# Conditioning tiles multiplied two stages earlier, norm rows loaded earlier, the decay chain later

## What is computed

```python
mod_lat = silu(c) @ w_ada + b_ada            # 12 tiles of 512 columns
mod_ctx = silu(c_ctx) @ w_ada + b_ada
sh_m, sc_m, gt_m, sh_f, sc_f, gt_f = split(mod_lat, 6)
u_ctx = ctx * (1 + csc_m) + csh_m            # only k and v are made of it
u_lat = x * (1 + sc_m) + sh_m
q, k, v, g, glu, gates = u_lat @ w_in + b_in
q, k = rope(q), rope(k)
# retention with decays exp(log_sigmoid(ret_decay)), state from k_c, v_c
y_a = (silu(g) * head_norm(o)) @ w_ret_out
z = silu(LN(depthwise_conv31(za * sigmoid(zb))))
y_b = z @ w_conv_out + b_conv_out
mix = (sigmoid(ga) * y_a + sigmoid(gb) * y_b) @ w_mix_out + b_mix_out
h = LN(ALPHA * x + gt_m * mix; ln1_g, ln1_b)
moe = sum over top 2 of 32 experts of (h * (1 + sc_f) + sh_f)
h = LN(ALPHA * h + gt_f * moe; ln2_g, ln2_b)
a_in = h * norm_pre_2 * row_scale            # into the second block
```

## Time and profile before

| | |
|---|---|
| median of 3 runs | 1579.76 us (1579.15 to 1589.21) |
| profiled execution | 1580.53 us, span 1578.7 us, mean granted clock 0.987 |
| PE busy | 1489.3 us (94%); weight loads 1030.8 |
| DVE, ACT, POOL busy | 715.5 (45%), 577.4 (37%), 415.5 (26%) |
| DMA | 381.18 MB, mean 241 GB/s |
| chain that ended last | PE 70%, DMA 12%, DVE 5%, POOL 4%, ACT 3% |

### The profile page before, as it was taken

The page is one execution under the profiler, slowest core; times in us unless marked ns, Lnnn a source line. Parts: engine busy times, 40 slices in busy tenths (PEclk is TensorE's granted clock), DMA queues, the critical chain, the costliest instruction groups (busy, mean ns, idle before and its releaser), DMA issues.

```text
span 1578.7 us, 22936 instructions
## 1 busy us (share of the span) xinstructions
PE 1489.3 (94%) x9454; PEld 1030.8 (65%) x9454; DVE 715.5 (45%) x1294; ACT 577.4 (37%) x781; POOL 415.5 (26%) x316
## 2 busy tenths in 40 slices
PE   5999999999999899999999999689999899999998
PEld 3788888888666544444443443268788678878786
DVE  2578887575545731212121111245522644344674
ACT  2441425454343311222121121234344355465553
POOL 0000000010000100000000000339887686757564
PEclk9999999999999999999999999899999999999999
DMA  9732224436788889999999999647456353443432
GB/s 325 238 101 87 81 80 154 134 106 217 251 307 319 309 354 427 427 427 428 428 428 429 428 430 426 242 142 230 153 184 209 129 174 119 133 134 131 137 107 94
DMA packets 107330, 381.18 MB, mean 241 GB/s; under 512 B 7782, under 2 KB 9614, under 8 KB 94958
## 3 DMA queue, kind: packets, MB, share of 16 engines
q1 hardware_dynamic: 107246, 380.02, 63.7%
HBM read 378.95 MB, written 1.05 MB: 241 GB/s over the span
## 4 chain that ended last, share of the span: by engine, by line
PE 70%; DMA 12%; DVE 5%; POOL 4%; ACT 3%; issue 1%; SPq 0%; DVEq 0%; ACTq 0%; POOLq 0%
PE ps L803 11%; PE ps L812 11%; PE ps L1228 11%; PE ps L804 10%; DMA arena<-in_w_exp_up 9%; PE ps L1238 4%; POOL w_lo L2474 3%; PE ps L996 3%; PE ps L995 3%; PE ps L1002 3%; PE ps L1249 2%; PE ps L886 2%; ACT w_hi L2556 1%; PE ps L1259 1%; PE ps L1395 1%
## 5 line engine op out<-in xcount | busy, mean ns | idle before, releaser
L2474 POOL TENSOR_TENSOR w_lo<-ring,w_hi 128x512 fp32r<-128x512 f32 x280 | 374.7, 1377 | 128.4 <-ACT w_hi L2556 116.8
L2556 ACT ACTIVATE w_hi<-ring 128x2048 fp32r<-128x2048 f32 x130 | 246.6, 1911 | 300.1 <-PE ps L812 129.2
L803 PE MATMUL ps<-w_hi,xt_hi 128*128 128x512 f32 x512 | 202.1, 395 | 1.8 <-ACT w_hi L2556 1.8
L804 PE MATMUL ps<-w_hi,xt_lo 128*128 128x512 f32 x480 | 187.0, 390 | 0.0
L1532 DVE TENSOR_TENSOR w_lo<-ring,w_hi 128x2048 fp32r<-128x2048 f32 x60 | 138.0, 2303 | 89.9 <-ACT w_hi L2556 89.6
L1228 PE MATMUL ps<-arena 128*32 128x512 f32 x1408 | 155.3, 593 | 7.4 <-DMA arena<-in_w_exp_up 6.3
L803 PE MATMUL ps<-w_hi,yt_hi 128*128 128x512 f32 x352 | 139.0, 395 | 4.7 <-issue 2.2
L812 PE MATMUL ps<-w_lo,xt_hi 128*128 128x512 f32 x512 | 127.3, 391 | 5.0 <-POOL w_lo L2474 4.9
L2462 POOL TENSOR_TENSOR arena<-arena 128x1024 f32<-128x1024 f32 x2 | 4.7, 2359 | 476.3 <-DMA arena<-in_ln_b 476.3
L1228 PEld LDWEIGHTS ps<-arena 128*32 128x32 f32 x1408 | 48.8, 110 | 111.0 <-issue 109.8
L2126 DVE TENSOR_SCALAR selT<-ps 128x256 fp32r<-128x256 f32 x32 | 13.6, 424 | 233.5 <-ACT arena L2892 233.5
(11 more groups left out here) (330 smaller groups left out, 2376.3 us busy)
## 6 DMA issues: line engine op xcount, KB each, us to landing
arena<-in_w_exp_gate SPq DMA_DIRECT2D x22, 2048.0 KB, 25.5
arena<-in_w_exp_up SPq DMA_DIRECT2D x22, 2048.0 KB, 30.0
arena<-in_w_exp_down SPq DMA_DIRECT2D x21, 2048.0 KB, 29.1
ring<-in_w_in SPq DMA_DIRECT2D x40, 1024.0 KB, 5.1
ring<-in_b_w_in SPq DMA_DIRECT2D x40, 1024.0 KB, 5.1
ring<-in_a_w_in SPq DMA_DIRECT2D x24, 1024.0 KB, 5.3
ring<-in_w_exp_down SPq DMA_DIRECT2D x11, 2048.0 KB, 28.1
ring<-in_w_exp_gate SPq DMA_DIRECT2D x10, 2048.0 KB, 25.5
```

The costliest lines, as they stand in the source:

```text
L803: pe.matmul(o[:, tt, :], hi[:, k, x_], w[:, c, :], start=(bias is None and j == 0 and c == 0), stop=False)
L804: pe.matmul(o[:, tt, :], lo[:, k, x_], w[:, c, :], start=False, stop=False)
L2474: ins = pool.tensor_tensor(w_lo2[:, slots_of[n], k, :], ring[:, slots_of[n], k, :], w[:, k, :].bitcast(F32), ALU.subtract)
L2556: act.activation(part_of(n)[1][:, :, :], ring[:, slots_of[n]], ACT.Copy).then_inc(S("w_hi_full"), 1)
```

## The change

- `MID_ORDER` puts the eight tail tiles between the k and v units, both units of a tile back to back (`tail_tile`); `OUT_ORDER` keeps only the 16 units of ret, conv and mix.
- Each tail tile's rows are copied by ACT (`tail_moved(t)`, a 128x512 copy) and the four rows that matter are moved by a DMA that ACT issues into `tail_rows`, 41 rows with the bias rows and a row of ones. In the output stage four `spread(c)` of two fp32 products each make all eight tiles of them, where there were eight `spread_tail`.
- The plan of pairs in the k/v stage is fixed: k_lat and v_lat in pair 2, k_ctx and v_ctx in pair 3, tail tiles, transposes and states in pairs 0 and 1.
- The decay chain on DVE starts behind `lo_of("glu", 3, 1)`, its two exponentials on ACT come behind `sigmoid_z(1)` and behind `turned_z(1)`; `modulate(1, 0)` and `gated(0)` come before it.
- ln2_g, ln2_b and norm_pre_2 are loaded behind the first experts' loads. POOL's `gain_products` goes; `mixer_input` makes the normed x in place and multiplies by norm_pre_2 with a third DVE instruction; `norm_x` goes. SP's loads for the second block wait for `a_in_ready` where they waited for `x_normed`.
- Places in memory, two bias loads less and three small loads more, and SP's waits ahead of two gain rows follow from that.

```diff
+MID_ORDER = [("k", 0, 0), ("k", 0, 1), ("tail", 0), ("k", 1, 0), ("k", 1, 1), ("tail", 1), ("v", 0, 0), ("tail", 2), ("v", 0, 1), ("tail", 3),
+             ("v", 1, 0), ("tail", 4), ("v", 1, 1), ("tail", 5), ("v", 2, 0), ("tail", 6), ("v", 2, 1), ("tail", 7), ("v", 3, 0), ("v", 3, 1)]
+
+OUT_ORDER = [("ret", t, j) for t in range(2) for j in range(4)] + [("conv", t, j) for t in range(2) for j in range(2)] + [("mix", t, j) for j in range(2) for t in range(2)]
...
-        take_next("k_lat0", "k_ctx0", ("zT", 1), "k_lat1", "k_ctx1", ("kT", 0))
-        take_next("v_lat0", "v_ctx0", ("kT", 1), "v_lat1", "v_ctx1", ("S", 0), "v_lat2", "v_ctx2", ("S", 1), "v_lat3", "v_ctx3", ("S", 2))
+        for i in range(2):
+            take("k_lat%d" % i, 2)
+            take("k_ctx%d" % i, 3)
+            take(("tail", i), 0)
+            take((("zT", 1), ("kT", 0))[i], 1)
+        for key, p in (("v_lat0", 2), ("v_ctx0", 3), (("tail", 2), 0), (("kT", 1), 1), (("tail", 3), 0), ("v_lat1", 2), ("v_ctx1", 3), (("tail", 4), 1),
+                       (("S", 0), 0), (("tail", 5), 1), ("v_lat2", 2), ("v_ctx2", 3), (("tail", 6), 0), (("S", 1), 1), (("tail", 7), 0),
+                       ("v_lat3", 2), ("v_ctx3", 3), (("S", 2), 1)):
+            take(key, p)
...
@@ first_experts (SP)
                 expert_load(1, 1, DOWN)
+                for v, name in ((ln2_g, "ln2_g"), (ln2_b, "ln2_b"), (pre0, "norm_pre_2")):
+                    sp.dma_start(v, a[name][0:1].broadcast_to([P, D])).then_inc(S("load_gains"), 16)
...
-                    sp.wait_ge(S("x_normed"), 1)
+                    sp.wait_ge(S("a_in_ready"), NT)
...
@@ PE
+            def spread(c):
...
+                o = claim(("spread", c))
+                for i in range(2):
+                    mm = pe.matmul(o[:, i, :], tail_pick[0:TAIL_ROWS, 2 * c + i:2 * c + i + 1].broadcast_to([TAIL_ROWS, P]), tail_rows, start=True, stop=True)
+                mm.then_inc(S("mod_spread"), 1)
+
+            def tail_tile(t):
+                o = claim(("tail", t))
+                for j in range(2):
+                    n = at_unit["tail", t, j]
+                    pe.wait_ge(S("w_full%d" % slots_of[n]), 16 * fills[n])
+                    row_products(o, j, s_cols, ring[:, slots_of[n]]).then_inc(S("unit_done"), 1)
...
             both_tile("k", 0)
+            tail_tile(0)
             turn_z(1)
             both_tile("k", 1)
+            tail_tile(1)
             turn_roped("k_roped", 0, ("kT", 0))
-            both_tile("v", 0)
+            both_unit("v", 0, 0)
+            tail_tile(2)
+            both_unit("v", 0, 1)
             turn_roped("k_roped", 1, ("kT", 1))
-            for t in range(1, 4):
-                both_tile("v", t)
-                context_state(t - 1)
+            tail_tile(3)
+            both_unit("v", 1, 0)
+            tail_tile(4)
+            both_unit("v", 1, 1)
+            context_state(0)
+            tail_tile(5)
+            both_unit("v", 2, 0)
...
@@ DVE, behind lo_of("glu", 3, 1)
+            conv_taps(6)
+            lo_of("k", 0, 0)
+            gated(1)
+            lo_of("k", 0, 1)
             dve.wait_ge(S("decay_exped"), 1)
...
+            conv_taps(12)
             dve.wait_ge(S("decay_exped"), 2)
             dve.tensor_scalar(wdec, wdec, DK ** -0.5, None, ALU.mult).then_inc(S("wdec_ready"), 1)
-            conv_taps(6)
-            lo_of("k", 0, 0)
-            gated(1)
-            lo_of("k", 0, 1)
-            conv_taps(20)
             lo_of("k", 1, 0)
             dve.wait_ge(S("load_rope"), 32)
             dve.wait_ge(S("lat_done"), 1)
...
             def mixer_input(tt):
-                link(dve.scalar_tensor_tensor(h_tok[:, tt, :], x[:, tt, :], mv[:, tt, 0:1], gain0, ALU.subtract, ALU.mult))
+                link(dve.scalar_tensor_tensor(x[:, tt, :], x[:, tt, :], mv[:, tt, 0:1], ln2_g, ALU.subtract, ALU.mult))
                 settle()
                 power_ready()
-                dve.scalar_tensor_tensor(h_tok[:, tt, :], h_tok[:, tt, :], rstd[:, tt:tt + 1], bias0, ALU.mult, ALU.add).then_inc(S("a_in_ready"), 1)
+                dve.scalar_tensor_tensor(x[:, tt, :], x[:, tt, :], rstd[:, tt:tt + 1], ln2_b, ALU.mult, ALU.add).then_inc(S("x_normed"), 1)
+                dve.wait_ge(S("x_normed"), tt + 1)
+                dve.tensor_tensor(h_tok[:, tt, :], x[:, tt, :], pre0, ALU.mult).then_inc(S("a_in_ready"), 1)
...
-            dve.wait_ge(S("gains_ready"), 2)
+            dve.wait_ge(S("load_gains"), 48)
...
@@ ACT
+            def tail_moved(t):
+
+                act.wait_ge(S("unit_done"), at_unit["tail", t, 1] + 1)
...
+                freed(act.activation(mod_rows[:, t % 2, :], buf(("tail", t))[:, 0, :], ACT.Copy), ("tail", t))
+                pair_evacuated(act, ("tail", t))
+                act.dma_start(tail_rows[4 * t:4 * t + 4], mod_rows[0:P:32, t % 2, :]).then_inc(S("tail_moved%d" % (t % 2)), 16)
...
             sigmoid_z(1)
+            act.wait_ge(S("decay_asked"), 1)
+            act.activation(la[:, 0, :], la[:, 0, :], ACT.Exp).then_inc(S("decay_exped"), 1)
             lead("k", 1, 0)
             lead("k", 1, 1)
             context_k(0)
+            tail_moved(0)
             turned_z(1)
+            act.wait_ge(S("decay_asked"), 2)
+            act.activation(wdec, wdec, ACT.Exp).then_inc(S("decay_exped"), 1)
             lead("v", 0, 0)
             lead("v", 0, 1)
             context_k(1)
+            tail_moved(1)
             turned_heads(0)
             lead("v", 1, 0)
+            tail_moved(2)
             lead("v", 1, 1)
             both_v(0)
             turned_heads(1)
+            tail_moved(3)
             decay_keys(0)
             decay_keys(1)
             lead("v", 2, 0)
+            tail_moved(4)
             lead("v", 2, 1)
             both_v(1)
             context_state(0)
+            tail_moved(5)
```

More of the change, by code:

```diff
@@ L250, in build @@
             stream_unit("glu", w_in, GLU[t], t, j)
-        for name in ("k", "v", "q", "g", "gate"):
+        for name, t, *half in MID_ORDER:
+            if name == "tail":
+                for j in range(2):
+                    stream_unit(name, a["w_ada"][0], 4 + t, t, j)
+            else:
+                stream_unit(name, w_in, IN_COLS[name][t], t, half[0])
+        for name in ("q", "g", "gate"):
             stream(name, w_in, IN_COLS[name], 2)
         for name, t, j in OUT_ORDER:
-            w = {"ret": "w_ret_out", "tail": "w_ada", "conv": "w_conv_out", "mix": "w_mix_out"}[name]
-            stream_unit(name, a[w][0], 4 + t if name == "tail" else t, t, j)
+            stream_unit(name, a["w_%s_out" % name][0], t, t, j)
         n_before = len(units)
@@ L626, in _ @@
             for part in range(2):
-                for name, b in (("in", a["b_in"]), ("tail", a["b_ada"][0:1, 2 * D:6 * D]), ("conv", a["b_conv_out"]), ("mix", a["b_mix_out"])):
+                for name, b in (("in", a["b_in"]), ("conv", a["b_conv_out"]), ("mix", a["b_mix_out"])):
                     r = 32 * part + BIAS_ROWS[name]
@@ L1915, in two @@
                 return v.rearrange("p (a b) -> p a b", a=2)
-            for t in range(2, 6):
-                pair_evacuated(dve, ("tail", t))
+            for c in range(1, 4):
+                pair_evacuated(dve, ("spread", c))
             ln1_g, ln1_b = gain_rows("ln1_g"), gain_rows("ln1_b")
@@ L2652, in _ @@
             lead("glu", 2, 1)
-            act.wait_ge(S("decay_asked"), 1)
-            act.activation(la[:, 0, :], la[:, 0, :], ACT.Exp).then_inc(S("decay_exped"), 1)
             sigmoid_z(0)
@@ L2659, in _ @@
             turned_z(0)
-            act.wait_ge(S("decay_asked"), 2)
-            act.activation(wdec, wdec, ACT.Exp).then_inc(S("decay_exped"), 1)
             evacuate_x(3)
@@ L2704, in _ @@
             context_state(3)
+            for i in range(2):
+                act.wait_ge(S("tail_moved%d" % i), 64)
             turned_heads(2)
@@ L2795, in _ @@
             lead("ret", 1, 1)
+            lead("ret", 1, 2)
+            lead("ret", 1, 3)
+            spread(0)
             spread(1)
-            lead("ret", 1, 2)
-            product_rows("tail", 2, 6)
+            lead("conv", 0, 0)
             spread(2)
-            lead("ret", 1, 3)
-            product_rows("tail", 3, 7)
-            lead("conv", 0, 0)
-            spread(3)
             for c in range(2):
@@ L2818, in _ @@
             lead("mix", 1, 1)
-            act.wait_ge(S("merged"), 2)
-            product_rows("tail", 6, 10)
-            spread(6)
             def h_lead(tt):
@@ L3045, in bias_columns, with tail_columns @@
     return out
+def tail_columns():
+    out = np.zeros((TAIL_ROWS, 8), np.float32)
+    for t in range(8):
+        out[4 * t:4 * t + 4, t] = 1
+        out[32 + t, t] = 1
+    out[40, 4:6] = 1
+    return out
 def tables():
```

250 lines of the change are left out of this document (104 added, 146 removed).

## The result

The changed kernel takes 1620.13 us (median of 4 runs, 1619.27 to 1626.32) beside 1579.67 for the kernel before: ratio 1.0252, 95% interval 1.0221 to 1.0284. It is slower by 40.5 us. The profiled execution took 1626.32 us (span 1624.4, before 1578.7). About 7 of these 45.7 us belong to one slow instruction in the attention's stage, told of at the end; a second profile (span 1617.0) doesn't have it.

The account below looks back on a forecast made before the run. PE was taken to bound the k/v stage, bytes the expert stage, and waits on loads and GpSimd the hand-over. Terms 64.3 − 3 − 20.7 − 1.5 + 3.7 − 14 = +28.8 on 1580.5 gave 1609.3 us, range 1590 to 1627.

Parts of the forecast that it names:

- the first wait: Before k's second tile PE waits for pair 2, held by the late second exponential and DVE's rope: 14.3 us.
- The waits at the pairs: k/v stage: PE waits for fixed pairs before k's second and all four v tiles: 14.3, 0.9 and 2.0, 9.2, 9.0, 2.7.
- v's second and third tile: k/v stage: copies stand behind leads waiting for loads; 9.2 us (up to 10.3) and 9.0 (8.1 to 9.7).
- The low clock: k/v stage: granted clock falls after PE stands still; 5 to 16 us, 11 taken.
- The price of the row products: k/v stage: eight conditioning tiles at 1.90 us of PE each, +15.2 us.
- The output stage: Ring-load waits go as row products leave; stage sum 101.6 us, so −20.7 (−18 to −22).
- Expert stage and hand-over: Norm rows add bytes to the expert stage, +3.7 us; the second block starts earlier, −14 (−11 to −15).
- the load of the fifth unit: Second block's ring load, started at 1046.11, goes out at about 1030; PE finishes that unit 11.3 us earlier.
- The front: Before the k/v stage: later decay chain removes idle and low clock ahead of the transposes, −3 us (−2 to −4).
- B: Rival, k/v stage: bank waits are hidden while PE multiplies tails, so −20.3, 1560 us; chance 0.12.
- C's case: Rival, k/v stage: only the decay chain's wait is real, with its clock, 14.3 + 4.3 on B, 1578 us; chance 0.08.
- D's loss: Rival, second block: hand-over's gain is swallowed by GpSimd's remainders or new loads, 1609 + 14 = 1623 us; chance 0.08.

Follow-up runs that it names:

- the two reorderings: On the changed kernel: ACT's copies and second decay exponential ahead of leads whose loads wait, 1571.26 us; that exponential alone directly behind lead(k,1,0), 1603.35 us.
- the mended order: The changed kernel with ACT's k/v-stage list reordered, copies and second decay exponential ahead of leads whose loads wait: 1571.26 us, ratio to the kernel before 0.9948.
- The part alone: The kernel before with only the norm rows loaded behind the first experts' loads, no GpSimd products, three-instruction mixer_input, SP's loads behind a_in_ready: 1571.71 us, ratio 0.9939.

## Why the prediction was right

The forecast was slower, 1609 with a range of 1590 to 1627; measured are 1620. The mechanism held: PE waits at the pairs, for the engines named, and the clock falls behind the waits. The sum was 11.7 short of the measured 40.5, and several terms came out beyond their own bounds; that 1620 is still within the range owes something to terms that erred the other way. (Added up again, the terms of the first wait give 14.2 where 14.3 stands, and the bounds of the stage 54.0 to 72.8 where 54.3 to 72.6 stands.)

*The waits at the pairs.* Predicted 14.3, 0.9 and 2.0, 9.2, 9.0, 2.7, in all 38.1; measured 13.05, 0.71 and 3.77, 10.29, 9.96, 2.79, in all 40.6. That they come from ACT's order and the late exponential, and not from the narrow plan of pairs as such, is shown by the two reorderings: all but 0.5 goes with the one, the first wait alone with the other. In the first wait two terms were wrong. ACT's issue of the tail's move was taken at 0.4, at most 0.6, and took 1.10. The other is the table load of 1.28. The trace of after has the load ahead of the first exponential (91.18) and none ahead of the second (121.80), with only copies between. The Trainium skill, ScalarE: Activation LUTs, section Table sets: the hidden batching unit, says that cheap functions such as copy are in every set; the trace agrees, and the further 1.4 us for a drain that the prediction gave by the page had nothing to apply to. In front of v's first context half the wait of 3.77 is above its bound of 3.5. In v's second and third tile the load of the waiting lead takes 7.35 and 7.0 us instead of 5.1, with the tail's loads issued just ahead of it: the upper ends of 10.3 and 9.7 were the better ones, and the third, 9.96, is above its own. A wait of 0.4 in front of tail 3's products wasn't in the sum.

*The low clock.* 11 had been taken, and it is 10.3, the difference of PE's busy time between the changed kernel and the mended order over the same products.

*The price of the row products.* 15.2 was predicted, eight times the 1.90 that a tile takes back to back. By PE's busy time it is 16.8 (325.6 for 308.7), 2.1 a tile: too low by 1.6.

*The output stage* is the term most mis-sized: −16.4 for −20.7, outside its bounds of −18 to −22. The load waits went, as said. Of the 105.9 us PE was idle for 3.7, where 1.8 had been put for copies and low clock: 1.19 ahead of the first conv product (at 520.64), where PE waits for DVE behind ACT's copies, and 2.46 ahead of a mix product (at 556.60), where ACT's list has its split of the unit, 1.91, behind the copy of the transposes, though ACT had stood idle for 9.49 us before it. In the kernel before, row products had stood in some of these places. The other 2.4 is PE's own time: 102.2 busy where the sum had 99.8 (the seven units from 467.31 to 506.01 are 5.53 apart, not 5.45).

*What moving the tails was worth.* Without its stalls, all tails in the k/v stage bring nothing: 1571.26 with all parts and the mended order, 1571.02 with tails left and the late exponential, 1567.54 with tails left and the early one. 16.8 us of PE time went from a stage with load waits into one that PE fills; the output stage gave back 14.8 (107.5 for 122.3) and the stretch behind the mix 1.7. Only with two tiles behind the mix does the move bring something: 1563.87 beside 1567.54, on the same chip.

*Expert stage and hand-over.* +4.4 for +3.7, −12.9 for −14. The part alone on the kernel before gave +4.8 and −11.0. PE's first transposes of the second block were to come 6.4 us earlier: they stand 44.4 us later than in the trace of before (1069.15 against 1024.75), where the expert stage's end stands 50.7 later, so 6.3. Counted from that end, the load of the fifth unit was to go out some 16 earlier, and went 11.7 earlier (1085.15 for 1046.11): SP's small loads ahead of it did go 16.2 earlier, but then its place in the ring was free only when PE had finished the block's first unit, at 1085.12. So PE had won 9.9 behind the fifth unit where 11.3 were predicted, and 3 more up to the 16th (2.7 predicted), where GpSimd's remainders had held it up before.

*The front* was −3.6 for −3; k's first bias row stands at 89.53 and 88.04 in two kernels that are the same up to there, so a part of it can be the execution's. Of the four rivals, B is what the mended order shows, at 1571 where it was put at 1560: its output stage begins 15.0 us later than in the kernel before (12.2 by B's terms) and takes 107.5 us (101.6 by them). C's case, the decay chain's wait alone, is in no run, and D's loss at the hand-over didn't occur.

The 11.7 that the sum was short: 3.8 from the k/v stage (1.6 of row products, 2.9 of idle, less 0.7 of clock), 4.3 from the output stage, 0.7 from the bytes, 1.1 from the hand-over, less 0.9 from the front and behind the mix, 9.0 together; about 1 more lies in the rest of the second block (the 8.0 of the table less 7), and what is left isn't placed.

## What to carry to other kernels

When a plan of accumulators is made narrower, read each engine's list for what stands ahead of the copy that frees one: a copy of 1 us behind a split that waits for a load of the latest freed slot costs the load, the split and the copy, here 10 us a tile. Put copies and small links of a chain ahead of instructions that wait for memory; here it cost no new wait and gave 49 us. Work that only fills should go where its engine already waits (two tiles behind the mix), and its result should not be asked for right behind a small transfer that runs beside bulk loads: 8 KB took 4.5 us there, and 0.4 with the DMA engines idle.

## What the runs showed of the hardware that was not expected

One DVE addition of two 128x1024 operands took 14.81 us in the first profile of the changed kernel, 1.22 at the same place in the second. Timelines of DVE and of GpSimd:

```profile
1315.41 14.81 DVE L2396 TENSOR_TENSOR arena<-arena 128x1024 f32<-128x1024 f32 x1
```

```profile
1314.22 14.92 POOL L2475 TENSOR_TENSOR w_lo<-ring,w_hi 128x512 fp32r<-128x512 f32 x12
```

GpSimd was in the middle of 28 subtractions without a gap, from 1292.27 to 1329.1 (the row holds the last twelve), and DVE's addition ended at 1330.2, when they had ended. PE then waited 6.26 us. In the second profile GpSimd's run is as unbroken, and the addition starts at 1315.24; there it is the subtraction beside it that is slow:

```profile
1315.34 2.27 POOL L2475 TENSOR_TENSOR w_lo<-ring,w_hi 128x512 fp32r<-128x512 f32 x1
```

Its neighbours take 1.3. The Trainium skill, SBUF — State Buffer, section Who interferes with whom, says that a DVE operation with two SBUF inputs and a GpSimd operation that reads SBUF exclude each other for a whole instruction. Both rows agree with the exclusion, but in the first DVE lost to twelve instructions in a row, not to one. It was seen in one execution, and no run was made to bring it about, so its cause is only argued.

A granted clock of 1.00 behind waits of 10 and 13 us, when they were filled with products of no use, was the other: the 4 us behind the first wait held 18 products instead of 9.
